# Turned probabilities of a pair of attention items: two ScalarE copies of 512 columns, or one of 1024

## The reference

```python
def memory_attention(q, mk, mv):
    n, t = q.shape[:2]
    s = jnp.einsum('nthd,nmhd->nhtm', q, mk).astype(jnp.float32) * (HEAD_DIM ** -0.5)
    p = jax.nn.softmax(s, axis=-1)
    o = jnp.einsum('nhtm,nmhd->nthd', p.astype(mv.dtype), mv)
    return o.reshape(n, t, X_WIDTH)
```

## Time and profile before

| | |
|---|---|
| median of 3 runs | 2313.45 us (2312.45 to 2313.55) |
| the profiled execution | 2310.54 us, of which 2308.8 are the span from its first to its last instruction |
| mean granted TensorE clock | 0.99 of full speed |
| busy: TensorE / its weight loads | 2265.2 us (98%) / 2165.7 us (94%) |
| busy: VectorE, ScalarE, GpSimd | 1117.8 (48%), 662.2 (29%), 552.0 (24%) |
| chain that ended last, by engine | TensorE 89%, VectorE 4%, issue 4%, ScalarE 2% |
| prompt attention of layer 0 and of layer 1 | about 218 to 342 us and 1412 to 1448 us |

### The profile page before, as it was taken

The page is one execution under the profiler, slowest core; times in us unless marked ns, Lnnn a source line. Parts: engine busy times, 40 slices in busy tenths (PEclk is TensorE's granted clock), DMA queues, the critical chain, the costliest instruction groups (busy, mean ns, idle before and its releaser), DMA issues.

```text
span 2308.8 us, 38804 instructions
## 1 busy us (share of the span) xinstructions
PE 2265.2 (98%) x15104; PEld 2165.7 (94%) x15104; DVE 1117.8 (48%) x2143; ACT 662.2 (29%) x1212; POOL 552.0 (24%) x412
## 2 busy tenths in 40 slices
PE   7998999999999999999999999999999999999999
PEld 6997679999999999999999986999999999999998
DVE  5325572464454554454561135335454555454554
ACT  6312792332111222211252225343211212212121
POOL 0002453322211222221252122342221222211221
PEclk9997999999999999999999998999999999999999
DMA  4224001111111111111111111111111111111112
GB/s 168 83 100 152 2 5 39 44 55 56 37 40 42 45 55 55 45 36 36 46 50 60 37 58 71 40 43 59 45 38 36 45 55 55 45 37 35 45 55 88
DMA packets 38855, 123.39 MB, mean 53 GB/s; under 512 B 5264, under 2 KB 13040, under 8 KB 37968
## 3 DMA queue, kind: packets, MB, share of 16 engines
q1 hardware_dynamic: 34656, 112.75, 15.0%
q10 hardware_dynamic: 4112, 9.43, 1.1%
HBM read 115.57 MB, written 8.63 MB: 54 GB/s over the span
## 4 chain that ended last, share of the span: by engine, by line
PE 89%; DVE 4%; issue 4%; ACT 2%; POOL 1%; DMA 0%; SPq 0%; ACTq 0%; DVEq 0%; POOLq 0%
PE ps L562 28%; PE ps L563 27%; PE ps L564 27%; PE ps L858 1%; PE ps L827 1%; PE ps L839 1%; DVE h_lo L1486 1%; PE ps L721 1%; DVE z L1888 1%; PE ps L906 1%; PE ps L708 1%; ACT s_exp L1240 1%; DMA x<-in_x_t 0%; POOL w_lo L432 0%; POOL ssq L447 0%
## 5 line engine op out<-in xcount | busy, mean ns | idle before, releaser
L562 PE MATMUL ps<-h_hi,w_hi 128*128 128x352 f32 x3120 | 1013.1, 325 | 17.2 <-DVE h_lo L1486 9.7
L563 PE MATMUL ps<-h_lo,w_hi 128*128 128x352 f32 x3120 | 1002.1, 321 | 0.0
L564 PE MATMUL ps<-h_hi,w_lo 128*128 128x352 f32 x3120 | 1001.7, 321 | 0.0
L432 POOL TENSOR_TENSOR w_lo<-raw,w_hi 128x1024 fp32r<-128x1024 f32 x118 | 296.4, 2512 | 1525.5 <-ACT w_hi L1050 1525.5
L562 PEld LDWEIGHTS ps<-h_hi,w_hi 128*128 128x128 f32 x3120 | 586.8, 188 | 36.3 <-issue 24.1
L563 PEld LDWEIGHTS ps<-h_lo,w_hi 128*128 128x128 f32 x3120 | 588.0, 188 | 0.0
L564 PEld LDWEIGHTS ps<-h_hi,w_lo 128*128 128x128 f32 x3120 | 586.3, 188 | 0.0
L1795 DVE TENSOR_TENSOR x<-x,ps 128x352 f32<-128x352 f32 x528 | 271.0, 520 | 173.5 <-PE ps L564 172.8
L562 PE MATMUL ps<-g_hi,d_hi 128*128 128x352 f32 x1056 | 340.4, 322 | 3.5 <-DVE g_lo L1788 3.5
L563 PE MATMUL ps<-g_lo,d_hi 128*128 128x352 f32 x1056 | 339.9, 322 | 0.0
L564 PE MATMUL ps<-g_hi,d_lo 128*128 128x352 f32 x1056 | 339.7, 322 | 0.0
(11 more groups left out here) (180 smaller groups left out, 1702.6 us busy)
## 6 DMA issues: line engine op xcount, KB each, us to landing
raw<-in_w SPq DMA_DIRECT2D x182, 512.0 KB, 3.5
out_y<-x ACTq DMA_DIRECT2D x8, 528.0 KB
s_mk<-in_s_mk SPq DMA_DIRECT2D x2, 2048.0 KB, 9.7
s_mv<-in_s_mv SPq DMA_DIRECT2D x2, 2048.0 KB, 13.8
x<-in_x_t SPq DMA_DIRECT2D x2, 1408.0 KB, 12.1
x<-in_x_t SPq DMA_DIRECT2D x2, 704.0 KB, 6.1
mem_x<-in_mem_t SPq DMA_DIRECT2D x1, 1024.0 KB, 7.4
s_k<-in_s_k SPq DMA_DIRECT2D x2, 512.0 KB, 4.2
```

The lines of the kernel that those rows point to most:

```text
L432: pool.tensor_tensor(lo, raw[:, slot], hi.bitcast(F32), ALU.subtract).then_inc(prepped, 1)
L562: pe.matmul(out, a, hi_x(k), start=(first and n == 0), stop=False)
L563: pe.matmul(out, a, lo_x(k), start=False, stop=False)
L564: ins = pe.matmul(out, b, hi_x(k), start=False, stop=(last and n == len(ks) - 1))
```

## The change

The two copies of a pair become one ScalarE instruction over banks 4 and 5 (1024 columns), which waits for the transposes of both items. `pturned_taken` then counts pairs: the values of both items wait for the pair's copy, and only the first transposes of a pair wait for the copy of the pair before. Where the first item has only half of its columns, the copy takes all 512 of its bank, the unused ones too, which nobody reads.

```diff
                 def turn(n):
                     kind, q, b = item(l, n)
                     pe.wait_ge(m["normed"], n + 1)
-                    if n >= 2:
-                        pe.wait_ge(m["pturned_taken"], n - 1)
+                    if n >= 2 and n % 2 == 0:
+                        pe.wait_ge(m["pturned_taken"], n // 2)
...
                 def values(n):
                     kind, q, b = item(l, n)
-                    pe.wait_ge(m["pturned_taken"], n + 1)
+                    pe.wait_ge(m["pturned_taken"], n // 2 + 1)
...
-                def take(n):
-                    kind, q, b = item(l, n)
-                    w0 = 2 * P if kind == "swa" and b == 0 else 0
-                    if n == 0 and l == 0:
+                def take(p):
+                    if p == 0 and l == 0:
                         act.wait_ge(v_stored, 16)
-                    act.wait_ge(m["pturned"], n + 1)
-                    if n >= 2:
-                        act.wait_ge(m["pv"], n // 2)
-                    scopy(pt[:, n % 2, w0:4 * P], ps[:, 4 + n % 2, w0:4 * P]).then_inc(m["pturned_taken"], 1)
+                    act.wait_ge(m["pturned"], 2 * p + 2)
+                    if p >= 1:
+                        act.wait_ge(m["pv"], p)
+                    scopy(pt[:, :, :], ps[:, 4:6, :]).then_inc(m["pturned_taken"], 1)
...
                 for it in range(M + 2):
                     if it >= 2:
-                        take(2 * (it - 2))
-                        take(2 * (it - 2) + 1)
+                        take(it - 2)
```

## The result

| | before | after |
|---|---|---|
| median | 2313.4 us | 2330.6 us (2325.2 to 2333.3) |
| profiled execution | 2310.54 us | 2328.41 us |
| span | 2308.8 us | 2326.7 us |

The ratio of the runs is 1.0076, with a 95% interval of 1.0061 to 1.0091: slower by 17 us (14 to 21). The forecast was 2339.5 us and a range from 2331 to 2346. A second measurement beside other runs of the kernel before, further down, gave 1.0093 (1.0076 to 1.0110), 21.5 us.

The account below looks back on a forecast made before the run. TensorE's instruction order was taken to bound attention. Over 40 pairs, 16.2 + 3.4 + 2.3 + 2.9 + 1.2 = 26.0 us of later values were added to the 2313.45 us median: 2339.5 us, range 2331 to 2346.

Parts of the forecast that it names:

- the restart of 0.04 for 31 pairs: TensorE's group of values takes 0.04 us longer after a stop, in 31 pairs that did not stop before: 1.2 us.
- the special pairs: Ten attention pairs with other waits or no scores between, each charged its own delay, together 2.9 us.
- The bound and the mechanism: In attention TensorE's order sets the pace; values then wait for a later, longer copy that the scores no longer cover.
- The first rival: ScalarE is the bound and merging relieves it: about 1.2 us saved, 2312.2 us; chance 0.03.
- (a) The start: Merged copy starts at T + 1.20 us, T being the start of the pair's transposes; the first copy started at T + 0.70.
- (b) The length: A ScalarE copy of 1024 columns takes 1.033 us, the bank edge costing nothing; bounds 1.00 to 1.17.
- (c) Release and restart: Values start 1.08 us after the merged copy's start, at T + 2.28; a stopped TensorE needs 0.04 more for its group.
- 21 window pairs: Pairs with window scores between transposes and values: 0.77 us lost each, 16.2 us.
- 5 memory pairs: Pairs with memory scores between transposes and values: 0.67 us lost each, 3.4 us.
- 4 at 0.49 in place of 0.57: Four pairs with memory scores between and a wait for exponentials after them: forecast 0.57 us each, 2.3 us.
- The return of 0.10 in the pairs with a wait for the exponentials: In memory attention TensorE's even scores stop waiting for exponentials, giving 0.10 us back in each of four pairs.
- The clock: Rival: TensorE's stops in attention lower its clock to 1.2 GHz, about 12 us more, 2351 us; chance 0.05.

Follow-up runs that it names:

- the second kernel above: Kernel before, still two copies of 512 columns, but each copy waits until both items are transposed; values wait for their own copy only: 1.0040.
- merged, more cover: Changed kernel with the next pair's first scores issued ahead of the values in 18 iterations of layer 0's window attention: 1.0070.
- before, shift alone: Kernel before plus 6 dummy identity transposes after the values in 18 iterations of layer 0, no copy merged: 1.0058.
- before, gate filled: Kernel before with dummy transposes where TensorE stands still around layer 1's gate: 0.9977, 2305.8 us.
- merged, gate filled: Changed kernel with dummy transposes where TensorE stands still around layer 1's gate: 2328.8 us.
- before, gate and start filled: Kernel before with dummy transposes around layer 1's gate, after 30 spreading products ahead of layer 0's attention and in its first two iterations: 1.0142.

## Why the prediction was right and wrong

**What failed, in short.** Two things of the sum. The loss in attention was put at 26.0 us and was 20.9: the start of the merged copy at T + 1.20 was T + 1.14, the restart of 0.04 for 31 pairs was nothing, the special pairs lost 0.8 less, and the short groups of values gave 0.4 back. And the clock outside attention was put at nothing, without a reason: the middle part became 3.5 us shorter in the profiled execution. The first alone would have left the forecast inside its range (2334.3); only with the second does the median fall below it.

**The bound and the mechanism: right.** TensorE's order set the pace, ScalarE at 99% did not, and the loss is values that wait for a merged copy with only 0.5 us of scores to cover it. Undoing one part at a time (T + 1.84, T + 1.79, T + 2.27) and adding cover (0.48 back) show it. The first rival, ScalarE as the bound, is out: the gain of one instruction for two exists, 0.06 us in a full pair, and is lost in a wait more than ten times as long. The forecast had 0.03; the mean over all pairs is 33 ns only by luck, since the unused columns of the five short pairs take part of the gain away. The Trainium skill (Perfetto Trace Analysis, section Optimizing Scalar/DVE Operations) says that breaking instructions up may let work be completed sooner where ScalarE or VectorE is not saturated but makes bubbles on other engines. Before the change ScalarE was saturated. The changed kernel is the case that the sentence describes, with ScalarE at 39.64 of 48.00 us and TensorE waiting 41.2 us for it, and there the trace agrees if the waits are broken up too: with two copies and single waits, which is the kernel before, attention is 20.9 us shorter. With two copies and both waits it is 1.3 longer.

**(a) The start: mis-sized, and the largest part of the error.** I wrote T + 1.20, by adding the spacing of two copies (0.50) to the start of the first. It is T + 1.14. The first copy starts at T + 0.70, so four more transposes take 0.44. The spacing of the copies was ScalarE's own pace; I had read 0.03 of it as a wait for the transposes. 0.06 a pair, some 2 us of the 5.

**(b) The length: right.** 1.024 for 1.033, and nothing for the bank's edge.

**(c) Release and restart: half wrong.** Values start 1.07 after the copy's start (I had 1.08). The restart of 0.04 does not exist. In the earlier trace rows the group took 1.07 because the values of item 1 had their own copy to wait for; the second kernel above, where this wait is left, has 1.07, and those without it have 1.02. I took a second wait for a cost of stopping. In the short pairs the merged kernel even gains: their values take 0.81 (303.80 to 304.61) in place of 0.90, since the second copy's wait is gone, 0.09 in four of them and 0.05 in one.

**The sum by terms:** 21 window pairs at 0.70 in place of 0.77, 14.7; 5 memory pairs at 0.59 in place of 0.67, 3.0; 4 at 0.49 in place of 0.57, 2.0; the special pairs 1.8 in place of 2.9 (of which 0.35 belong to the very first one, which lost 0.41 but is not in the 1.8, behind a start that happened to be 0.42 earlier); restarts 0 in place of 1.2; short groups -0.4. Together 21.0 against 20.9 measured in attention and 26.0 forecast. The return of 0.10 in the pairs with a wait for the exponentials came as written.

**The clock: treated on one side only.** I let it cost, with a chance of 0.05, and only inside attention, where behind the first pair it stayed at 1.00 in every kernel. That a shift by itself moves how long TensorE stays at 1.2 GHz somewhere else, in either direction, was in no rival. In the first profile the middle part gave 3.5 us back, 3.4 of them clock, and the rest took 0.6: that leads from 2310.54 + 20.9 = 2331.4 to 2328.41. By the right sizes alone the forecast would have been 2334.3 for the median, inside the range. The trace of before has 6.8 us withheld around the gate, which a shift could give back; a range down to 2334.3 - 6.8 = 2327.5 was what it called for. Had the changed kernel kept the low clock of the one before, the time would have lain inside the range with the same errors in attention behind it.

**What stays open.** Two measurements of the change give 17 us (14 to 21) and 21 us (18 to 25), and runs at the same granted clock 20 to 21. They agree with 20.9 from attention and a few microseconds of clock either way. Whether the changed kernel keeps a mean gain of 1 or 2 us in the middle part over many runs can't be told from 9 runs, nor what decides, at the same standstill, whether and for how long the clock falls.

## What to carry to other kernels

Before two hand-offs are merged into one, work out how much later the data come: by the rest of the producer's work (here 0.44 us, from T + 0.70 to T + 1.14) plus the other half of the copy (0.44). Only the consumer's other work in that place counts as cover, here 0.5 us of scores out of the 1.2 between the end of the transposes and the values. A full engine is no proof that it is the pace; read the consumer's starts, and if its steps follow each other without a gap, saving on its supplier gains nothing. And take the release of an instruction from a row in which its engine was waiting, not from one in which it was busy.

## What the runs showed of the hardware

The parts of the profiled executions, in us, with what the granted clock withheld in the middle part:

| kernel | attention 0 | attention 1 | middle | withheld | of it ahead of a wait | middle less the rest |
|---|---|---|---|---|---|---|
| before | 109.94 | 26.25 | 1080.58 | 8.5 | 1.7 | 1073.8 |
| values wait for both | 116.71 | 27.38 | 1080.64 | 8.5 | 1.7 | 1073.8 |
| copies wait for both | 117.46 | 28.27 | 1076.89 | 5.1 | 1.7 | 1073.5 |
| both waits, two copies | 127.55 | 30.88 | 1077.14 | 5.1 | 1.7 | 1073.7 |
| merged | 126.70 | 30.39 | 1077.04 | 5.1 | 1.7 | 1073.6 |
| merged, once more | 126.70 | 30.39 | 1075.88 | 3.4 | 0 | 1072.5 |
| merged in layer 1 | 110.40 | 30.38 | 1080.12 | 6.8 | 0 | 1073.3 |
| merged in layer 0 | 126.71 | 26.25 | 1073.92 | 1.7 | 1.7 | 1073.9 |
| merged, more cover | 120.93 | 30.38 | 1079.74 | 6.8 | 0 | 1072.9 |
| before, shift alone | 123.42 | 26.24 | 1077.12 | 3.4 | 0 | 1073.7 |
| before, gate filled | 110.39 | 26.25 | 1073.48 | 0 | 0 | 1073.5 |
| merged, gate filled | 126.70 | 30.39 | 1077.58 | 3.4 | 0 | 1074.2 |
| before, gate and start filled | 110.11 | 26.25 | 1076.41 | 5.1 | 1.7 | 1073.0 |

The 1.7 us are the early fall where it lies ahead of the wait for GpSimd and costs nothing. For the same code attention repeats to 0.02 us in layer 1 and to half a microsecond in layer 0, where in some executions the first pair still runs at 1.2 GHz. The middle part, which no edit touches but the fillings of the gate, varies by 7 us, and less the clock that counts by 1.7: most of the variation is time at 1.2 GHz. The early fall shows that low clock costs only where TensorE is the pace.

Of that clock the rows show this much. Ahead of the gate TensorE stands still for 0.88 and 1.3 to 1.9 us in all ten executions without filling; in nine its clock then falls, for 6.8 to 13.7 us, in one (merged in layer 0) it does not. After the gate it falls in two of the thirteen. With the gate filled it falls in two of three, for 3.4 and 6.8 us. The filling was worth 0.23% of the kernel before, over 10 runs. So where and how long the clock falls is not set by the edit alone, and a few per mille between two kernels that shift TensorE's standstills should be checked against the granted clock before they are explained by the edit.
